# The weight and bias of a layer norm, moved across the mixing over positions

## What is computed

```python
def layernorm(x, g, b):
    xf = x.astype(jnp.float32)
    mu = jnp.mean(xf, axis=-1, keepdims=True)
    xc = xf - mu
    y = xc * lax.rsqrt(jnp.mean(xc * xc, axis=-1, keepdims=True) + EPS)
    return (y * g.astype(jnp.float32) + b.astype(jnp.float32)).astype(x.dtype)

def gmlp_branch(zu, zv, ln_g, ln_b, w_s, b_s):
    u = jax.nn.gelu(zu, approximate=False)
    v = layernorm(jax.nn.gelu(zv, approximate=False), ln_g, ln_b)
    v = v.reshape(B, nb, GMLP_BLOCK, GMLP_GROUPS, GMLP_GROUP_DIM)
    w = jnp.where(chunk_causal_mask(GMLP_BLOCK)[None], w_s, 0).astype(v.dtype)
    mixed = jnp.einsum('gqp,bnpgc->bnqgc', w, v) + b_s.T.astype(v.dtype)[None, None, :, :, None]
    return u * mixed.reshape(B, S, GMLP_WIDTH)
```

## Time and profile before

| what | us |
|---|---|
| median of three runs | 2180.22 |
| lowest and highest | 2179.78, 2184.69 |
| the profiled execution | 2182.87 |
| its span in the profile | 2181.1 |
| TensorE busy in it | 2129.5 |
| VectorE, ScalarE, GpSimd busy | 975.4, 794.3, 853.0 |

### The profile page before, as it was taken

One profiled execution on the slowest core, in us unless ns is written; L12 is line 12 of the kernel. 1 busy time (PEld: TensorE's weight loads), 2 busy tenths in 40 slices (PEclk: granted clock), 3 DMA queues, 4 the chain that ended last, 5 costly groups with the idle time before them and its releaser, 6 DMA issues.

```text
span 2181.1 us, 23934 instructions
## 1 busy us (share of the span) xinstructions
PE 2129.5 (98%) x9438; PEld 1713.1 (79%) x9438; DVE 975.4 (45%) x1634; ACT 794.3 (36%) x1135; POOL 853.0 (39%) x357
## 2 busy tenths in 40 slices
PE   6799999999999999999999999998999999999999
PEld 5688888878888888888888888877656668888887
DVE  4678878433221324344552424422544545524242
ACT  5354544534222225323332222443454443322222
POOL 3333333544444444434444443533211114444444
PEclk9999999999999999999999999999999999999999
DMA  4122222342323222322223232322101112323323
GB/s 169 63 74 78 71 85 78 107 139 94 102 92 104 97 90 97 98 96 97 87 98 98 98 103 92 116 87 83 49 29 39 39 39 87 98 97 97 105 91 112
DMA packets 54975, 194.76 MB, mean 89 GB/s; under 512 B 6096, under 2 KB 6224, under 8 KB 54864
## 3 DMA queue, kind: packets, MB, share of 16 engines
q1 hardware_dynamic: 54864, 193.23, 26.8%
HBM read 191.11 MB, written 2.10 MB: 89 GB/s over the span
## 4 chain that ended last, share of the span: by engine, by line
PE 94%; DVE 3%; ACT 1%; issue 1%; DMA 0%; SPq 0%; POOL 0%; DVEq 0%; POOLq 0%
PE ps L1239 28%; PE ps L1241 28%; PE ps L1240 28%; PE ps L1485 2%; PE ps L1508 2%; PE ps L1247 1%; PE ps L1317 1%; PE ps L1487 0%; PE ps L1516 0%; PE ps L1499 0%; PE ps L1339 0%; PE ps L1303 0%; DVE arena L1183 0%; DVE arena L706 0%; DMA w_raw<-in_panels 0%
## 5 line engine op out<-in xcount | busy, mean ns | idle before, releaser
L318 POOL TENSOR_TENSOR w_lo<-w_raw,w_hi 128x1024 fp32r<-128x1024 f32 x353 | 852.8, 2418 | 1316.0 <-ACT w_hi L335 1309.3
L1239 PE MATMUL ps<-x_hi,w_hi 128*128 128x512 f32 x1864 | 749.8, 402 | 20.2 <-POOL w_lo L318 9.2
L1241 PE MATMUL ps<-x_hi,w_lo 128*128 128x512 f32 x1864 | 731.6, 392 | 0.0
L1240 PE MATMUL ps<-x_lo,w_hi 128*128 128x512 f32 x1864 | 731.2, 392 | 0.0
L335 ACT CAST w_hi<-w_raw 128x1024 fp32r<-128x1024 f32 x353 | 366.3, 1041 | 332.4 <-PE ps L1241 325.6
L1239 PEld LDWEIGHTS ps<-x_hi,w_hi 128*128 128x128 f32 x1864 | 353.9, 190 | 99.8 <-issue 17.9
L1240 PEld LDWEIGHTS ps<-x_lo,w_hi 128*128 128x128 f32 x1864 | 353.9, 190 | 78.7 <-issue 7.2
L1241 PEld LDWEIGHTS ps<-x_hi,w_lo 128*128 128x128 f32 x1864 | 353.1, 189 | 74.7
L695 DVE TENSOR_TENSOR arena<-ps,inv_rms 128x512 f32<-128x512 f32 x208 | 143.5, 690 | 481.1 <-PE ps L1241 461.3
L1239 PE MATMUL ps<-hid_hi,w_hi 128*128 128x512 f32 x864 | 338.4, 392 | 5.4 <-DVE hid_lo L724 5.3
L1240 PE MATMUL ps<-hid_lo,w_hi 128*128 128x512 f32 x864 | 337.5, 391 | 0.0
(11 more groups left out here) (165 smaller groups left out, 1494.7 us busy)
## 6 DMA issues: line engine op xcount, KB each, us to landing
w_raw<-in_panels SPq DMA_DIRECT2D x353, 512.0 KB, 3.5
x<-in_xT SPq DMA_DIRECT2D x16, 256.0 KB, 2.7
outT<-x SPq DMA_DIRECT2D x8, 256.0 KB, 2.0
arena<-in_rows SPq DMA_DIRECT2D x1, 768.0 KB, 9.4
consts<-in_const SPq DMA_DIRECT2D x1, 664.5 KB, 7.4
arena<-in_ws SPq DMA_DIRECT2D x1, 256.0 KB, 9.7
params<-in_param SPq DMA_DIRECT2D x1, 112.0 KB, 2.1
```

The source lines that it names most:

```text
L318: nc.gpsimd.tensor_tensor(w_lo[:, p % RING, :], w_raw[:, p % RING, :], w_hi[:, p % RING, :].bitcast(F), ALU.subtract).then_inc(w_low, 1)
L1239: nc.tensor.matmul(o, wh, hi[:, kt, :], start=(kt == 0), stop=False)
L1240: nc.tensor.matmul(o, wh, lo[:, kt, :], start=False, stop=False)
L1241: ins = nc.tensor.matmul(o, wl, hi[:, kt, :], start=False, stop=(kt == tiles - 1))
```

## The change

The weight and the bias of the layer norm come as columns of the parameters (`gain("ln_g", gr)`, `gain("ln_b", gr)`), one column for each group of channels, since behind the mixing channels lie on partitions. `layer_norm` keeps its tensor_scalar alone and no longer waits inside. TensorE multiplies ones with the masked spatial weights once, behind the transposes, into bank 7: that is the sum of each row of weights, on all partitions. `gmlp_bias`, on VectorE behind `layer_norm(3)`, makes of it the new bias: four instructions, one for each group. `gmlp_out` multiplies the mixed value by the weight and adds that bias in one instruction. Three rows in the transfer of `rows` become one.

```diff
-        rows_sb, ws_sb, vn = y[:, 0:3, :], y[:, 3, :].rearrange("p (a n) -> p a n", a=GROUPS), y[:, 4:8, :]
+        rows_sb, mix_bias, ws_sb, vn = y[:, 0, :], y[:, 1, :], y[:, 3, :].rearrange("p (a n) -> p a n", a=GROUPS), y[:, 4:8, :]
...
             def layer_norm(b):
 
-                link(v.tensor_scalar(vn[:, b, :], ps[:, 2 + b, :], ln_mv[:, b, 0:1], ln_inv[:, b:b + 1],
-                                     ALU.subtract, ALU.mult))
-                link(v.tensor_tensor(vn[:, b, :], vn[:, b, :], lng, ALU.mult))
-                v.tensor_tensor(vn[:, b, :], vn[:, b, :], lnb, ALU.add).then_inc(v_normed, 1)
+                v.tensor_scalar(vn[:, b, :], ps[:, 2 + b, :], ln_mv[:, b, 0:1], ln_inv[:, b:b + 1],
+                                ALU.subtract, ALU.mult).then_inc(v_normed, 1)
+
+            def gmlp_bias():
+
+
+                dve.wait_ge(ws_summed, 1)
+                for gr in range(GROUPS):
+                    at = slice(gr * P, (gr + 1) * P)
+                    steps.done(v.scalar_tensor_tensor(mix_bias[:, at], ps[:, 7, at], gain("ln_b", gr), rows_sb[:, at],
+                                                      ALU.mult, ALU.add))
+                steps.wait()
...
-                bias = bs[:, gr * P:(gr + 1) * P].unsqueeze(1).broadcast_to([P, BLK, P])
-                v.tensor_tensor(zv[:, gr, :].rearrange("p (b n) -> p b n", b=BLK),
-                                ps[:, 2 + gr, :].rearrange("p (b n) -> p b n", b=BLK),
-                                bias, ALU.add).then_inc(mixed_read, 1)
+                bias = mix_bias[:, gr * P:(gr + 1) * P].unsqueeze(1).broadcast_to([P, BLK, P])
+                v.scalar_tensor_tensor(zv[:, gr, :].rearrange("p (b n) -> p b n", b=BLK),
+                                       ps[:, 2 + gr, :].rearrange("p (b n) -> p b n", b=BLK),
+                                       gain("ln_g", gr), bias, ALU.mult, ALU.add).then_inc(mixed_read, 1)
...
                     if h == 0:
                         layer_norm(2)
                         layer_norm(3)
+                        gmlp_bias()
...
             def mix():
 
-                pe.wait_ge(ws_masked, 1)
                 pe.wait_ge(v_normed, BLK)
...
                 if h == 0:
                     for b in range(BLK):
                         turn_zv(b)
+                    pe.wait_ge(ws_masked, 1)
+                    nc.tensor.matmul(ps[:, 7, :], c("ones"), ws_sb[:, :, :], start=True, stop=True).then_inc(ws_summed, 1)
...
-    rows = np.stack([i["gmlp_ln_g"][0], i["gmlp_ln_b"][0], i["gmlp_bs"][0].reshape(-1)])
+    rows = i["gmlp_bs"][0].reshape(-1)
```

## The result

The changed kernel takes 2170.96 us, the median of five runs (2170.47 to 2172.70); the kernel before took 2184.00 beside it (five runs, 2179.78 to 2185.31). The ratio is 0.9948, with a 95% interval from 0.9937 to 0.9959: 11.4 us at 2184 (9.0 to 13.8 by the interval), faster by 0.5%. The time lies in the predicted range, 2.2 us above the forecast of 2168.8. The profiled execution took 2170.47 us, its span is 2168.7.

What follows compares the result with a forecast made beforehand. TensorE was taken as the bound, with three first-head gaps waiting for VectorE. Terms 2.90 + 6.78 + 1.90 - 0.2 = 11.4 us took the profiled 2182.87 to 2171.5, and 2.65 lower for the median gave 2168.8; range 2166.8 to 2172.5.

Steps and rivals of the forecast that it cites:

- First two blocks: Layer norm in head 0: two tensor_scalars without a wait take 1.44 us instead of 4.34, saving 2.90 us.
- Rival (b): First blocks' gain lost if GpSimd's subtraction holding VectorE at line 926 didn't move: gain 8.5, 2171.7 us, chance 0.06.
- Last two blocks: Layer norm ahead of the mixing: 1.53 us instead of 8.31, saving 6.78 us, 3.9 of it stalls.
- The mixing: TensorE's 32 passes over positions at full clock: 3.56 us instead of 5.46, saving 1.90 us.
- rival (a): Lower clock comes back at the mixing, which takes 5.46 us again: gain 9.68, time 2170.5 us, chance 0.27.
- The matmul of ones: Added on TensorE behind the transposes: 0.86 us, costing nothing while a gap of about 1.8 us remains.
- The late eviction: VectorE's eviction of the panel ahead of the mixing, behind bias and stalled multiplications, at 86.4: 0.2 us lost.
- The outputs of the mixing: Four scalar_tensor_tensors with PSUM and one SBUF input: priced like line 770, no stall beside GpSimd; 1.1 us lost otherwise.
- The sum, 11.4: Head 0's total gain: 2.90 + 6.78 + 1.90 - 0.2 = 11.4 us, what follows starting earlier as a whole.
- (c): Gain given back later by VectorE in the heads: time about 2180 us, chance 0.07.
- (d): Slower: moved work in the attention part meets the clock worse, 2185 us at 0.88 granted; chance 0.03.
- (e): More gain than summed, by one low clock stretch fewer elsewhere, some 1.5 us: 2167.3 us, chance 0.05.

Runs made afterwards that it cites:

- the run with the steps put back: Changed kernel with two idle VectorE steps put back behind each of the layer norm's first two tensor_scalars: 2173.32 us, ratio 0.9956 to the kernel before.
- the run with the bias later: Changed kernel with the new bias made behind the eviction of the panel ahead of the mixing: 2170.18 us, ratio 0.9944 to the kernel before.
- the runs with two SBUF inputs: Changed kernel with two idle two-SBUF-input steps put back behind each of the last two tensor_scalars: 2180.81 us, ratio 0.9989 to the kernel before.
- with one in PSUM: Changed kernel with idle steps behind each of the last two tensor_scalars, each reading PSUM and one SBUF input: 2176.35 us, ratio 0.9967 to before.
- the kernel with the three moves: Changed kernel with tensor_scalars, eviction of the head's values and eviction of panel p + 4 moved earlier or later in VectorE's order: 2166.14 us, ratio 0.9918 to before.

## Where the prediction held, and the step that failed

- **What bounds the kernel: right.** The three gaps were VectorE's; two are short now and one is gone.
- **First two blocks, 2.90 us: right.** Line 754 to the eviction takes 60.38 - 58.95 = 1.43, predicted 1.44, and the run with the steps put back gave 2.93. Rival (b) is out: GpSimd's subtraction that holds VectorE up began at 64.07 instead of 67.21, 2.90 earlier against the first eviction.
- **Last two blocks, 6.78 us: right.** From the first eviction to the mixing it is 27.77 us after and 37.56 before, 9.79 for both halves, predicted 9.68. The 3.9 us of stalls in it were measured apart, at 3.89.
- **The mixing, 1.90 us: right in kind, 0.28 too much.** The clock stayed at 1.00, so rival (a) didn't happen. This had been a choice between two gaps of nearly one length, one with the low clock behind it and one without, and not something worked out. The size was wrong by a mix of two measures. Before and after, the panel behind the mixing starts here:

```profile
92.30 0.48 PE L1239 MATMUL ps<-x_hi,w_hi 128*128 128x512 f32 x1
```

```profile
80.65 0.48 PE L1248 MATMUL ps<-x_hi,w_hi 128*128 128x512 f32 x1
```

From the start of the mixing that is 5.22 us before (92.30 - 87.08) and 3.60 after (80.65 - 77.05): 1.62 won. The 3.56 of the prediction, a time from pass to pass, was right to 0.04; but it was taken off 5.46, the duration of a whole row, whose last 0.24 us lie beside the next panel.

- **The matmul of ones: right**, hidden in a gap of 1.62 (predicted 1.8).
- **The late eviction: right in size, 0.15** by the run with the bias later. The stalls behind the bias came as described: 6.85 for the seven multiplications. The eviction ended at 85.44 + 0.68 = 86.12, with 0.24 for the earlier start 86.36, predicted 86.4.
- **The outputs of the mixing: right**, 2.71 for four, no stall beside GpSimd, as the Trainium skill (SBUF — State Buffer, Who interferes with whom) has it for one SBUF input; the runs with two SBUF inputs (2.52 and 2.73 us) and with one in PSUM (0.69) agree with both halves of that rule.
- **The sum, 11.4: right.** 9.79 + 1.62 - 0.15 = 11.26, measured 11.25 in the distance. It came this close in part because the layer norm's 0.11 too little and the mixing's 0.28 too much stand against each other.
- **Two readings were off, and no term hangs on them.** The panel ahead of the mixing ended at 79.82 + 0.39 = 80.21, not at about 80.05; and the eviction at 49.52 ended at 50.21, 0.02 behind the subtraction in which it was said to lie.
- **The time, 2168.8: 2.2 too low. The step that failed is the last one**, "The median of the three runs is 2.65 lower". The sum made against the profiled execution gave 2171.5; the changed kernel took 2170.47 when profiled and 2170.96 as a median. The 2.65 were taken, with no reason given, for something that the profiled execution has on top. They were scatter: of the 38 runs of the kernel before that are known now, 9 lie between 2179.2 and 2181.0 and 29 between 2182.7 and 2185.3, and two of the three known then were of the 9. The median of the 38 is 2183.5, so the profiled execution, 2182.87, had nothing on top. What makes a run of this kernel a low one stays open; its one profile isn't of such a run. Within the sum, the one term off by more than 0.2 us is the mixing, above.
- **Where luck helped.** That the ratio gives the sum's 11.4 us is in part luck: its interval goes from 9.0 to 13.8, the second measurement (0.9943) gives 12.4 at 2183.4, and the medians differ by 13.0. The distance shows the gain, not these. Nor does the time decide between the rivals: 2170.96 lies nearer to the 2170.5 of rival (a) than to the forecast, and only the clock of 1.00 in the mixing rules (a) out.
- **Rivals (c), (d) and (e)** didn't happen, by the changed kernel's second profile: the rest took 2064.1 us, as before. A low stretch fewer, as in (e), is seen in five profiles of other kernels.

## What to carry to other kernels

Before an instruction is priced by its own duration, look at what it runs beside and what waits behind it: here eight instructions of 0.7 us were worth 9.8 us of TensorE's time and 1.6 us by its clock, because two of them stood behind GpSimd and all of them ahead of an event for which TensorE waited. A good part of such a gain can be had by order alone, by placing the work in time in which its engine waits for another. And where a few runs scatter, leave the sum against the profiled execution as it is; don't correct it by a median of three.

## What the runs showed of the hardware that was not expected

GpSimd doesn't always win against VectorE. In the changed kernel its subtraction at 78.11, issued just after the first of the seven multiplications had started, waited for that one (2.61 us instead of 2.4) and then held up the second. In the kernel with the three moves one was issued in the eighth of sixteen VectorE instructions with two SBUF inputs that follow each other without a pause, and waited for the last of them to end:

```profile
68.12 5.29 POOL L319 TENSOR_TENSOR w_lo<-w_raw,w_hi 128x1024 fp32r<-128x1024 f32 x1 [2.84 <-ACT w_hi L336]
```

It ended at 73.41, 2.3 us behind the end of the sixteen at 71.1; none of those that followed its issue was stalled. The same is seen with the bias later, where it came in the fourth of eight (6.46 for two). But in the kernel with the three moves the next one but one came in the second of the seven multiplications, went next, and held up the third (GpSimd's row, then VectorE's):

```profile
77.08 2.45 POOL L319 TENSOR_TENSOR w_lo<-w_raw,w_hi 128x1024 fp32r<-128x1024 f32 x1 [0.42 <-ACT w_hi L336]
```

```profile
77.20 2.61 DVE L868 TENSOR_TENSOR arena<-arena 128x256 f32<-128x256 f32 x1
```

In head 0 of all these profiles, a subtraction that came in the first or second instruction of such a run waited less than 0.5 us, and one that came in the fourth or eighth waited for the end of the run, 1.7 to 2.9 us. What decides it was not tried.

The clock did not fall behind the gaps of 1.42 to 1.65 us in head 0 in any of the profiles, and it fell behind all of those of 2.85 us and more there (2.85, 2.86, 4.51, 4.56, 6.87, 8.37). In between it did either: not behind 2.29, and behind the 2.20 us gap of the later stage in seven profiles of twelve. So the length of the gap alone doesn't tell.
